# Short convolutions and a value copy moved in a two-layer hybrid decoder step: VectorE's order around the 31-tap convolutions

## What is computed

```python
z = rmsnorm(h, g_mix) @ w_in
# A: gated short convolution, width 3, 384 channels
y_a = gate_b * causal_dwconv(gate_c * xa, prev_a, w_conv_a)
# B: chunked spatial gating, 256 channels
u, v = gelu(z_u), layernorm(gelu(z_v))
y_b = u * chunk_mix(v, w_s, b_s)
# C: GLU, causal depthwise convolution of width 31, LayerNorm, swish, 384 channels
y_c = silu(layernorm(causal_dwconv(glu, prev_c, w_conv_c) + b_conv_c))
h = h + concat(rmsnorm(y_a), rmsnorm(y_b), rmsnorm(y_c)) @ w_o
# then a feed-forward part (dense in layer 0, top 2 of 8 experts in layer 1),
# an input embedding (p @ w_ple_proj) gated by a projection, and a final norm
```

## Time and profile before

| | |
|---|---|
| median of 3 runs | 1107.47 us (1107.23 to 1108.84) |
| the profiled execution | 1108.74 us, its span 1107.1 us |
| TensorE busy (matmuls) | 1074.6 us, 97% of the span |
| VectorE busy | 891.9 us, 81% |
| ScalarE busy | 670.1 us, 61% |
| granted TensorE clock over the span | 0.993 |

### The profile page before, as it was taken

One profiled execution on the slowest core, in us unless ns is written; L12 is line 12 of the kernel. 1 busy time (PEld: TensorE's weight loads), 2 busy tenths in 40 slices (PEclk: granted clock), 3 DMA queues, 4 the chain that ended last, 5 costly groups with the idle time before them and its releaser, 6 DMA issues.

```text
span 1107.1 us, 16194 instructions
## 1 busy us (share of the span) xinstructions
PE 1074.6 (97%) x5881; PEld 928.3 (84%) x5881; DVE 891.9 (81%) x1257; ACT 670.1 (61%) x840; POOL 43.5 (4%) x58
## 2 busy tenths in 40 slices
PE   7998999999999998899999999999999999999996
PEld 5887899999999887788888888888888888878785
DVE  3898566556667799758989989899898998999785
ACT  2104344444445112638888788888888888888674
POOL 1000000000000000000000000000100001002000
PEclk9999999999999999899999999999999999999998
DMA  7442544654452442437999999999999999999920
GB/s 309 167 152 78 188 175 171 236 187 152 170 211 77 168 152 78 153 115 299 369 354 404 368 383 369 359 415 358 378 378 354 410 359 384 380 369 403 376 83 40
DMA packets 23909, 291.50 MB, mean 263 GB/s; under 512 B 3128, under 2 KB 3160, under 8 KB 6960
## 3 DMA queue, kind: packets, MB, share of 16 engines
q1 hardware_dynamic: 20752, 280.32, 65.9%
q0 software_dynamic: 3104, 10.46, 2.7%
HBM read 283.98 MB, written 6.79 MB: 263 GB/s over the span
## 4 chain that ended last, share of the span: by engine, by line
PE 92%; DVE 3%; ACT 2%; DMA 2%; issue 1%; DVEq 0%; ACTq 0%
PE bank L658 16%; PE bank L662 15%; PE bank L661 15%; PE bank L702 14%; PE bank L726 8%; PE bank L729 8%; PE bank L730 8%; PE bank L742 3%; DMA ring<-wstream 1%; PE bank L602 1%; DVE rstd L1363 1%; PE bank L586 1%; PE bank L567 1%; DMA h<-x_in 0%; DVE wlo L1258 0%
## 5 line engine op out<-in xcount | busy, mean ns | idle before, releaser
L1258 DVE TENSOR_TENSOR wlo<-ring,whi 128x1024 fp32r<-128x1024 f32 x384 | 460.1, 1221 | 50.3 <-ACT whi L869 42.5
L869 ACT ACTIVATE whi<-ring 128x1024 fp32r<-128x1024 f32 x384 | 404.0, 1059 | 86.8 <-PE bank L658 68.9
L658 PE MATMUL bank<-whi,gh_hi 128*128 128x512 f32 x512 | 204.5, 399 | 0.1
L662 PE MATMUL bank<-whi,gh_lo 128*128 128x512 f32 x512 | 199.8, 390 | 0.0
L661 PE MATMUL bank<-wlo,gh_hi 128*128 128x512 f32 x512 | 199.6, 390 | 0.0
L726 PE MATMUL bank<-gh_hi,whi 128*128 128x264 f32 x480 | 138.0, 288 | 0.1
L729 PE MATMUL bank<-gh_lo,whi 128*128 128x264 f32 x480 | 136.0, 283 | 0.0
L730 PE MATMUL bank<-gh_hi,wlo 128*128 128x264 f32 x480 | 135.9, 283 | 0.0
L658 PEld LDWEIGHTS bank<-whi,gh_hi 128*128 128x128 f32 x512 | 96.2, 188 | 22.3 <-DVE wlo L1258 3.9
L662 PEld LDWEIGHTS bank<-whi,gh_lo 128*128 128x128 f32 x512 | 96.1, 188 | 20.9
L950 ACT ACTIVATE whi<-ring 128x1024 fp32r<-128x1024 f32 x87 | 91.2, 1050 | 36.3 <-PE bank L726 28.7
(11 more groups left out here) (250 smaller groups left out, 1369.9 us busy)
## 6 DMA issues: line engine op xcount, KB each, us to landing
ring<-wstream SPq DMA_DIRECT2D x131, 2048.0 KB, 8.8
y_rows<-work POOLq DMA_DIRECT2D x7, 512.0 KB, 8.2
h<-x_in SPq DMA_DIRECT2D x1, 1056.0 KB, 4.9
y_out<-work SPq DMA_DIRECT2D x2, 528.0 KB, 3.0
xn_rows<-work SPq DMA_DIRECT2D x2, 512.5 KB
par<-par_in SPq DMA_DIRECT2D x2, 494.5 KB, 7.7
c_sample<-xc POOLq DMA_DIRECT2D x2, 372.0 KB, 3.7
stc<-state_in SPq DMA_DIRECT2D x2, 360.0 KB, 9.3
```

The source lines that it names most:

```text
L658: mm = pe.matmul(out[:, :], xh, whi[:, pos, cols_], start=(k == 0), stop=False)
L662: mm = pe.matmul(out[:, :], xl, whi[:, pos, cols_], start=False, stop=(k == last))
L869: nc.scalar.activation(whi[:, q % SPLITS, :], quarter_at(q), ACT.Copy).then_inc(S["hi"], 1)
L1258: v.tensor_tensor(wlo[:, q % SPLITS, :], quarter_at(q), whi[:, q % SPLITS, :].bitcast(F32), ALU.subtract).then_inc(S["lo"], 1)
```

## The change

Four edits, all in the mixer, in both layers:

- `some_taps` chooses the chunk with the fewest taps done, and not the one that it chose last if another is open, in place of the fixed turn.
- The width-3 convolution of a chunk of A is made in the loop over the pairs as soon as its `apad` rows are there (`convolve_a`), with a tap behind each of its first four instructions, into a buffer of its own (`near`), and is multiplied by `rstd` there. A round issues 3 + 3 + 4 + 2 taps in place of 3 + 3 + 5.
- `mix_a` then is one instruction: the PSUM bank of gate_b times `near`, which is the evacuation too. `y_a` is signalled by an empty instruction behind a wait for all of them.
- The copy of the transposed value rows from bank 5 into `vtok` moves from VectorE, behind the centring, to ScalarE, ahead of the second high half and of the embedding rows.

```diff
--- before.py
+++ after.py
@@ -1007,6 +1007,9 @@
                 for c in range(2 * CB + 2, N_ZAB):
                     high_upto(dense_quarters(B["zab"] + c))
 
+                act.wait_ge(S["vt"], 1)
+                nc.scalar.activation(vtok[:, :, :].rearrange("p j d -> p (j d)"), bank[5][:, :], ACT.Copy).then_inc(
+                    S["vtok"], 1)
                 high_upto(dense_quarters(B["pp"] + BANKS - 1))
                 for k in range(BANKS):
                     embedding_rows(l, k)
@@ -1395,20 +1398,18 @@
 
                 wc = cols(l, "w_conv_c").rearrange("p (c k) -> p c k", k=TAPS_C)
                 last = [0] * CC
-                taps_left = [iter(range(TAPS_C)) for _ in range(CC)]
-                turn_of = [0]
+                taps_done = [0] * CC
+                newest = [None]
 
                 def some_taps(n, chunks=CC):
 
-                    missed = 0
-                    while n and missed < chunks:
-                        c = turn_of[0] % chunks
-                        turn_of[0] += 1
-                        k = next(taps_left[c], None)
-                        if k is None:
-                            missed += 1
-                            continue
-                        n, missed = n - 1, 0
+                    for _ in range(n):
+                        open_chunks = [c for c in range(chunks) if taps_done[c] < TAPS_C]
+                        if not open_chunks:
+                            return
+                        c = min(open_chunks, key=lambda c: (c == newest[0], taps_done[c]))
+                        k, newest[0] = taps_done[c], c
+                        taps_done[c] += 1
                         src, dst = cpad[:, c, k:k + SEQ], cv[:, c, 0:SEQ]
                         if k == 0:
                             last[c] = tick(nc.vector.tensor_scalar(dst, src, wc[:, c, 0:1], col(l, "b_conv_c", c),
@@ -1463,6 +1464,20 @@
 
                 wa = cols(l, "w_conv_a").rearrange("p (c k) -> p c k", k=TAPS_A)
                 at = B["zab"] + 2 * CB
+                near = [up[:, 0, :], up[:, 1, :], pp[:, 5, :]]
+
+                def convolve_a(c):
+                    for k in range(TAPS_A):
+                        src, dst = apad[:, c, k:k + SEQ], near[c][:, 0:SEQ]
+                        link(nc.vector.tensor_scalar(dst, src, wa[:, c, 0:1], None, ALU.mult) if k == 0 else
+                             nc.vector.scalar_tensor_tensor(dst, src, wa[:, c, k:k + 1], dst, ALU.mult, ALU.add))
+                        some_taps(1)
+                    pv = prod[:, 0:NB * TAPS_A].rearrange("p (b k) -> p b k", k=TAPS_A)
+                    link(nc.vector.tensor_tensor(pv, xa[:, c], wa[:, c, :].unsqueeze(1).to_broadcast([P, NB, TAPS_A]),
+                                                 ALU.mult))
+                    some_taps(1)
+                    link(nc.vector.tensor_reduce(near[c][:, SEQ:T], pv, AX_X, ALU.add))
+                    link(nc.vector.tensor_tensor(near[c], near[c], rstd[:, :], ALU.mult))
 
                 dve.wait_ge(S["gelu"], 2 * CB)
                 for c in range(CA):
@@ -1474,7 +1489,8 @@
                     dve.wait_ge(acc_evac, at + 2 * c + 2)
                     nc.vector.tensor_tensor(apad[:, c, TAPS_A - 1:], pp[:, 6, 0:SEQ], pp[:, 7, 0:SEQ], ALU.mult)
                     link(nc.vector.tensor_tensor(xa[:, c, :, TAPS_A - 1], pp[:, 6, SEQ:T], pp[:, 7, SEQ:T], ALU.mult))
-                    some_taps(5)
+                    convolve_a(c)
+                    some_taps(2)
                     if c:
                         low_upto(dense_quarters(at + 2 * c + 1))
                     if c == 0:
@@ -1484,21 +1500,12 @@
                             [P, CB, T]), ALU.mult).then_inc(S["scaled"], 1)
                         low_upto(dense_quarters(at + 1))
                 def mix_a(c):
-                    evacuate(at + 2 * CA + c, ycat[:, c, :])
-                    for k in range(TAPS_A):
-                        src, dst = apad[:, c, k:k + SEQ], up[:, 0, 0:SEQ]
-                        link(nc.vector.tensor_scalar(dst, src, wa[:, c, 0:1], None, ALU.mult) if k == 0 else
-                             nc.vector.scalar_tensor_tensor(dst, src, wa[:, c, k:k + 1], dst, ALU.mult, ALU.add))
-                    pv = prod[:, 0:NB * TAPS_A].rearrange("p (b k) -> p b k", k=TAPS_A)
-                    link(nc.vector.tensor_tensor(pv, xa[:, c], wa[:, c, :].unsqueeze(1).to_broadcast([P, NB, TAPS_A]),
-                                                 ALU.mult))
-                    link(nc.vector.tensor_reduce(up[:, 0, SEQ:T], pv, AX_X, ALU.add))
-                    dve.wait_ge(acc_evac, at + 2 * CA + c + 1)
-                    i = nc.vector.tensor_tensor(ycat[:, c, :], ycat[:, c, :], up[:, 0, :], ALU.mult)
+                    dve.wait_ge(acc_ready, at + 2 * CA + c + 1)
+                    nc.vector.tensor_tensor(ycat[:, c, :], bank[(at + 2 * CA + c) % BANKS][:, 0:T], near[c],
+                                            ALU.mult).then_inc(acc_evac, 1)
                     if c == CA - 1:
-                        i.then_inc(S["y_a"], 1)
-                    else:
-                        link(i)
+                        dve.wait_ge(acc_evac, at + 3 * CA)
+                        dve.nop().then_inc(S["y_a"], 1)
                     low_upto(dense_quarters(at + 2 * CA + c))
 
 
@@ -1511,9 +1518,6 @@
                 nc.vector.tensor_tensor(cv[:, :, :], cv[:, :, :], bank[4][:, 0:T].unsqueeze(1).to_broadcast([P, CC, T]),
                                         ALU.subtract).then_inc(S["centred"], 1)
 
-                dve.wait_ge(S["vt"], 1)
-                nc.vector.tensor_copy(vtok[:, :, :], bank[5][:, :].rearrange("p (j d) -> p j d", j=CHUNKS)).then_inc(
-                    S["vtok"], 1)
                 low_upto(dense_quarters(B["pp"] + BANKS - 1))
                 mix_a(CA - 1)
                 low_upto(splits(NEED[B["pp"] + KD - 1]))
```

## The result

The changed kernel takes 1110.1 us (median of 10 runs, 1109.12 to 1111.29) beside 1107.78 us of the kernel before on the same chip (10 runs, 1105.94 to 1108.84): a ratio of 1.0023, 95% interval 1.0014 to 1.0031, which is slower by 2.3 us. 1110.2 was forecast. The profiled execution took 1110.15 us, its span 1108.5.

The account below looks back on a forecast made before the run. TensorE's chain was taken as the bound, VectorE mattering only where TensorE waits. Taps 5.10 us later (6.96 - 1.10 - 0.76) lose 1.91 us in layer 0 and 0.82 in layer 1: 1107.47 + 2.73 = 1110.2 us, range 1108.2 to 1112.2.

Parts of the forecast that it names:

- The margin: Layer 0: the sum of taps is ready 3.23 us before TensorE takes it; made 5.10 us later, it loses 1.91.
- The convolution's 2.32 us: VectorE's gate loop: each early `convolve_a` keeps its old price of 2.32 us, 6.96 us per layer for three.
- the bounds: Limits on convolutions interleaved with taps: the layer's sum 0.75 us smaller or 1.26 us larger; neither was taken.
- The lower bound: Six three-operand convolution steps per layer cost 0.395 us each, not 0.52; the layer's sum is 0.75 us smaller.
- the rival of the cheaper convolutions: Taps come only 4.35 us late, losing 1.16 us in layer 0 and 0.07 in layer 1: 1108.7 us; chance 0.23.
- Idle taken up, 1.10 us: VectorE's gate loop: idle of 0.34 and 0.76 us per layer goes, because later work finds its chunks ready.
- Dealing, 0.76 us: The last nine taps, dealt over chunks, take 3.64 us in place of 4.40, 0.76 us less per layer.
- the rival in which dealing saves nothing: The last taps keep their 0.76 us in both layers: 4.25 us lost, 1111.7 us; chance 0.10.
- the fallen clock: Layer 0: the new 1.9 us wait halves TensorE's clock for 6.7 us, costing 3.4 us more: 1113.6; chance 0.06.
- Layer 1: Average starts at 429.32, fourth embedding chunk at 434.49 after evacuation at 434.44: 0.82 us lost; waits of 1.9 and 1.0 us.
- ScalarE's copy: Value-row copy takes 597 ns on ScalarE; the second high half behind it slips, hidden by 2.4 us of cover.
- The other side: Convolutions add 3.2 us or less: layer 0 loses nothing, layer 1 sheds its 2.09 us wait: 1105.4 us; chance 0.06.

Follow-up runs that it names:

- e5: Changed kernel with two of three short convolutions early, the third behind `sample_taps` and two evacuations, ahead of the centring: 1107.68 us, ratio 1.0002.
- e9: Kernel before with only the dealing of taps and ScalarE's copy of the value rows; convolutions and evacuations unmoved: 1106.91 us, ratio 0.9991.
- e8: Changed kernel with each `convolve_a` wait put off to just ahead of the reading step, one tap moved: 1106.66 us, ratio 0.9995.
- e3: Kernel before with the dealing of taps alone: 1108.68 us, one run.
- e2: Changed kernel with the old fixed turn of taps over the chunks in place of the dealing: 1111.97 us, one run.
- e7: e6, with ScalarE squaring group A's rows ahead of the root of C's variance: 1104.95 us, ratio 0.9992.
- e1: Changed kernel with the three short convolutions back behind the sum of the taps, in `mix_a`; other parts kept: 1112.35 us, ratio 1.0050.
- e6: e5, with `mix_a(2)` ahead of the centring and two low halves behind it: 1105.98 us, ratio 0.9987.
- e11: Kernel before with six idle fp32 matmuls behind the norm of C in layer 1: 1106.95 us, ratio 0.9990.

## Why the prediction was right

*The margin.* 3.23 us, and 5.10 us to go into it: shown by e5, where 2.78 us fit and nothing is lost, and by e9, where the convolutions stay and nothing is lost. The averages start at 85.66 us; counted from the first projection that is 85.66 + 0.20 = 85.86 on the scale of before, 1.78 us later than 84.08 where 1.91 was forecast, and the stage lost just that, 1.79: what was lost there was carried to the end. The wait reads 1.62 us and not 1.78, since it is counted from the end of the last transpose, and before the averages began 0.16 us ahead of that end (83.64 + 0.60 = 84.24). The transposes of before, ahead of the first row:

```profile
83.64 0.60 PE L766 MATMUL bank<-ident,lnb 128*128 128x128 f32 x4
```

The sum of the taps itself is complete at 85.42 + 0.18 = 85.60, 85.80 on the scale of before: 4.95 us later, where 5.10 was forecast.

*The convolution's 2.32 us.* Measured 2.31, beside taps that keep their 0.40 us. The choice between the bounds was right for the stated reason: the links keep a tap from filling a pause. The lower bound, the rival of the cheaper convolutions, is a real case once the waits are moved (e8), and it was set too high: some 0.7 us per convolution went there, where the bound took off 0.75 for all three.

*Idle taken up, 1.10 us.* The idle rows in the later loop are gone.

*Dealing, 0.76 us.* Right for the kernel before (e3: 4.40 to 3.65), and the sum needed only that the last taps run at 0.40 us, which they do. But as a term of its own it was mis-sized: undone in the changed kernel it adds 0.25 us of wait a layer (e2), so by its waits the rival in which dealing saves nothing would have cost 0.5 us in all and not 1.5. That e2 comes near this rival's 1111.7 us all the same is the fallen clock's doing. The page of the Trainium skill that was weighed there (VectorE: DVE Perf Modes) measured copies with a semaphore behind each and behind the last alone (The DRAIN you can't avoid), and advises to count operations and not semaphores (Rules for kernel authors). That count does not tell e8 from the changed kernel, which has the same operations and signals and takes some 3 us more (ratios of 0.9995 and 1.0023 to the kernel before): what counts in these rows is where the waits stand.

*Layer 1.* Forecast 429.32, 434.44 and a loss of 0.82. This stage starts 355.33 - 353.74 = 1.59 us later, so on the scale of before the average started at 429.18 and the fourth chunk at 434.47: 0.80 us lost. The two pieces were to be 1.9 and 1.0 us and are 1.62 and 1.01; the wait ahead of the centring 0.8 and is 1.01. The 0.98 us of the stage table have 0.18 more. They lie behind the first row of the output projection: from there to the end of the stage are 486.07 - 450.45 = 35.62 us before and 488.64 - 452.83 = 35.81 now, in rows that the prediction did not reckon with. What causes them was not tested.

*ScalarE's copy.* 0.60 us in both layers, and the high halves behind it end well ahead of their use. ScalarE in order of time, layer 1:

```profile
429.19 0.60 ACT L1011 ACTIVATE vtok<-bank 128x512 f32<-128x512 f32 x1 [13.13 <-PE bank L766]
429.69 1.05 ACT L950 ACTIVATE whi<-ring 128x1024 fp32r<-128x1024 f32 x1
```

They end at 430.74 and the low halves that need them start at 433.31 (above): the cover of some 2.5 us was there.

*The rivals.* The clock did not fall in layer 0: it is 1.00 in every stretch from 80 to 134 us. Two of the stretches of layer 1's output projection that ran at half speed before, now:

```profile
452.00:454.00 2.00, 1.17 (x6) 1.17 (x7) 1.97 (x2) 1.73 (x6) 0.00 (x0) 0.79 1.03 442
...
456.00:458.00 2.00, 2.00 (x11) 2.00 (x10) 0.77 (x3) 1.40 (x2) 1.09 (x2) 0.50 0.00 0
```

From 452 to 460 the four stretches have 0.79, 0.50, 0.50 and 0.51, so the time at 0.50 is 0.84 + 4.00 + 1.96 = 6.8 us, as before. But the reason given against the fallen clock, that the new wait is shorter than the one that left the clock alone, does not hold: in e2 a wait of 1.87 us, shorter than the 2.09, brought it to 0.50 in layer 0. That cost 5.37 - 3.72 = 1.65 us, about half of the 3.4 that the rival had. The forecast had a wait of 1.9 us there, and 1.62 came; that the clock held is measured, but no reason for it is shown, and in this the forecast was lucky.

The other side was mis-sized too: it let layer 1 shed all of its 2.09 us if the taps came in time. In e8 and e9 they do, and 1.0 and 1.1 us of wait ahead of the fourth chunk stay, since the centring and the low halves still stand ahead of its evacuation; e8 took 1106.66 us, not 1105.4.

## What to carry to other kernels

Work that moves ahead of a result spends that result's margin: find the margin in the consumer's row before moving, and move no more than fits. When an instruction does two things at once (free a bank and use another operand), the slower operand decides when the bank is free. A pause is filled by independent work only if the wait is written ahead of the reader and not behind the writer; and a stall that is released by a busy engine may be only that engine's order of work.

## What was not expected

A halved clock makes a stall's cost depend on more than its length. In the profiles of this study the output projection of layer 1 ran at 0.50 for 6.8 us in some kernels (before, changed, e2, e7 to e9) and for 3.4 us in others (e1, e3, e5, e6), with a wait of 2.7 to 2.9 us ahead of it in each. In e1, e5 and e6 the first nine matmuls behind that wait still ran at full speed, and the fall came with the next wait, of 1.25 us. The difference is worth up to 1.7 us of a run and lies in none of the edits. Nor does the length of a wait alone decide whether the clock falls: 1.87 us did it in layer 0 of e2, and 1.88 us in its layer 1 and 2.09 us in the kernel before did not. What decides was not settled, and there is one profile of each kernel.

Removing a stall can also be given back at once: the half speed in the kernel before hid all but 0.3 us of a wait for VectorE's low rows that is 1.3 us without it (e11).
